# Moving the last expert's up projection ahead of the down projection before it, in a routed mixture stage on one Trainium2 core

## The reference

```
aff  = softmax(t @ w_r);  gate, idx = top_k(aff.T, cap)
xe   = t[idx]
hid  = silu(xe @ w_gate[e]) * (xe @ w_up[e])
ye   = (hid @ w_down[e]) * gate
out  = zeros.at[idx].add(ye)
```

## Time and profile before

| | |
|---|---|
| median of 3 runs | 2408.3 us (2407.99 to 2409.02) |
| profiled execution, first to last instruction | 2406.4 us |
| TensorE busy | 2205.8 us |
| VectorE busy | 1613.7 us |
| ScalarE busy | 1261.6 us |
| mean granted TensorE clock | 0.957 of full |

### The profile page before, as it was taken

One profiled execution on the slowest core, in us unless ns is written; L12 is line 12 of the kernel. 1 busy time (PEld: TensorE's weight loads), 2 busy tenths in 40 slices (PEclk: granted clock), 3 DMA queues, 4 the chain that ended last, 5 costly groups with the idle time before them and its releaser, 6 DMA issues. The chain is left out here.

```text
span 2406.4 us, 32340 instructions
## 1 busy us (share of the span) xinstructions
PE 2205.8 (92%) x11028; PEld 1677.9 (70%) x11028; DVE 1613.7 (67%) x1832; ACT 1261.6 (52%) x1486; POOL 545.4 (23%) x430
## 2 busy tenths in 40 slices
PE   8899998969999999977899999969969999999993
PEld 5677776747777777746788888757756777777772
DVE  3566664578888888855566566552258888888883
ACT  3444443157777777743443434341107777777772
POOL 1100000012234233205232222200000332344222
PEclk9999998979999999987999999989979999999997
DMA  7000004769999999934111112152169999999983
GB/s 264 1 14 8 13 14 156 280 228 378 385 385 378 396 382 383 351 95 135 36 49 49 49 48 61 56 191 88 70 245 342 382 381 389 390 380 383 393 295 126
DMA packets 169530, 520.40 MB, mean 216 GB/s; under 512 B 11808, under 2 KB 49440, under 8 KB 169184
## 3 DMA queue, kind: packets, MB, share of 16 engines
q1 hardware_dynamic: 162272, 494.05, 54.4%
q0 software_dynamic: 7168, 25.17, 4.5%
HBM read 481.43 MB, written 37.75 MB: 216 GB/s over the span
## 5 line engine op out<-in xcount | busy, mean ns | idle before, releaser
L1764 DVE TENSOR_TENSOR m_w_lo<-s_raw,m_w_hi 128x2048 fp32r<-128x2048 f32 x384 | 865.9, 2288 | 144.6 <-ACT m_w_hi L1713 143.0
L1713 ACT ACTIVATE m_w_hi<-s_raw 128x2048 fp32r<-128x2048 f32 x384 | 731.1, 1916 | 175.9 <-PE m_ps_down L1809 77.3
L1807 PE MATMUL m_ps_gate<-m_w_hi,m_xeT_hi 128*96 128x512 f32 x512 | 206.0, 402 | 3.8 <-DVE m_xeT_lo L1770 3.8
L1807 PE MATMUL m_ps_down<-m_w_hi,m_hidT_hi 128*96 128x512 f32 x512 | 203.9, 398 | 3.8 <-DVE m_hidT_lo L1770 3.8
L1809 PE MATMUL m_ps_gate<-m_w_hi,m_xeT_lo 128*96 128x512 f32 x512 | 204.3, 399 | 0.0
L1809 PE MATMUL m_ps_down<-m_w_hi,m_hidT_lo 128*96 128x512 f32 x512 | 204.1, 399 | 0.0
L1807 PE MATMUL m_ps_up<-m_w_hi,m_xeT_hi 128*96 128x512 f32 x512 | 203.9, 398 | 0.0
L1684 POOL DMA_INDIRECT acc<-m_ye,m_row_scatter x32 | 47.0, 1469 | 688.4 <-ACT m_ye L1730 688.4
L1809 PE MATMUL m_ps_up<-m_w_hi,m_xeT_lo 128*96 128x512 f32 x512 | 202.7, 396 | 0.0
L1808 PE MATMUL m_ps_gate<-m_w_lo,m_xeT_hi 128*96 128x512 f32 x512 | 202.5, 395 | 0.0
L1808 PE MATMUL m_ps_down<-m_w_lo,m_hidT_hi 128*96 128x512 f32 x512 | 202.3, 395 | 0.0
(11 more groups left out here) (228 smaller groups left out, 4200.4 us busy)
## 6 DMA issues: line engine op xcount, KB each, us to landing
s_raw<-in_w_gate SPq DMA_DIRECT2D x128, 1024.0 KB, 7.6
s_raw<-in_w_up SPq DMA_DIRECT2D x128, 1024.0 KB, 7.3
s_raw<-in_w_down SPq DMA_DIRECT2D x128, 1024.0 KB, 7.8
s_raw<-in_w_qkv_b SPq DMA_DIRECT2D x16, 512.0 KB, 5.8
s_raw<-in_w_qkv_b SPq DMA_DIRECT2D x32, 256.0 KB, 6.1
s_raw<-in_w_o_b SPq DMA_DIRECT2D x1, 8192.0 KB, 23.2
acc<-o_x SPq DMA_DIRECT2D x12, 512.0 KB, 2.6
xn<-o_xn SPq DMA_DIRECT2D x12, 512.0 KB, 3.0
```

The lines of the kernel that those rows point to most:

```text
L1713: act.activation(hi[:, split, :, :].rearrange("p k n -> p (k n)"), raw[:, slot, :], ACT.Copy).then_inc(hi_ready, 1)
L1764: dve.tensor_tensor(lo[:, split, :, :].rearrange("p k n -> p (k n)"), raw[:, slot, :], hi[:, split, :, :].rearrange("p k n -> p (k n)"), A ...
L1807: pe.matmul(out[:, cols], left_hi[:, k, :], hi[:, split, kk, cols], start=(k == 0), stop=False)
```

## The change

The order of the pieces at the end becomes: up 14, gate 15, up 15, down 14, down 15. Expert 14's list has 16 pieces now and expert 15's four. The gate is already one expert ahead, so up 15 uses the same transposed tokens as gate 15 did. `hid` of expert 15 is made on VectorE behind the split of place 13 of that list (the second piece of down 14); TensorE transposes it ahead of place 14, and ScalarE and VectorE evacuate it behind the split of place 14. The transposed `hid` of expert 14 is still in use by then, so that of expert 15 goes to the buffer of the transposed tokens of parity 0, and down 15 reads it there. `down_out(14)` keeps its place index 3 in the list of expert 15, which now is the fourth piece of down 15. The loads follow the new order: up 15 ahead of down 14, and down 15 when the pieces of down 14 have been split. Both layers have the change.

```diff
+        def before_last(e):
+            return isinstance(e, int) and e == LAST - 1
+        UP, GATE, DOWN = list(range(0, 4)), list(range(4, 8)), list(range(8, 12))
         def pieces(e):
-            slots = [0, 1, 2, 3, 8, 9, 10, 11] if is_last(e) else list(range(SLOTS))
-            return list(enumerate(slots))
+            slots = UP + GATE + (UP if before_last(e) else []) + DOWN
+            return list(enumerate(DOWN if is_last(e) else slots))
         def q_of(e, place):
-            return e * SLOTS + 4 + place
+            return e * SLOTS + 4 + place + (4 if is_last(e) else 0)
...
                 for j in range(4):
                     wait_low(sp, e - 1, j)
                     load(e, io.w_up, j, 0)
-                if not is_last(e):
+                for j in range(4):
+                    wait_low(sp, e - 1, 4 + j)
+                    load(e + 1, io.w_gate, j, 4)
+                if before_last(e):
                     for j in range(4):
-                        wait_low(sp, e - 1, 4 + j)
-                        load(e + 1, io.w_gate, j, 4)
+                        wait_low(sp, e, j)
+                        load(LAST, io.w_up, j, 0)
                 for j in range(4):
                     wait_low(sp, e - 1, 8 + j)
                     load(e, io.w_down, j, 8)
-            with sp.Fori(1, LAST) as e:
+            with sp.Fori(1, LAST - 1) as e:
                 step(e)
-            step(LAST)
+            step(LAST - 1)
+            for j in range(4):
+                wait_low(sp, LAST - 1, 12 + j)
+                load(LAST, io.w_down, j, 8)
...
@@ ScalarE
-                    ahead = 1 if 4 <= slot < 8 else 0
+                    ahead = 1 if 4 <= slot < 8 or (slot < 4 and place >= 8) else 0
                     high(q_of(e, place), (4 + place) % SPLITS, slot, (e + ahead) * 16 + base + 16)
...
-                    if place == (5 if is_last(e) else 8):
-                        turned(hidT_hi[:, :, :], e * 2 + (2 if is_last(e) else 3))
+                    if place == 8:
+                        turned(hidT_hi[:, :, :], e * 2 + 3)
                     if place == 10:
                         gate_out(e + 1, q_of(e, 8))
+                    if before_last(e) and place == 14:
+                        turned(xeT_hi[:, 0, :, :], 2 * EXPERTS)
                 if is_last(e):
-                    down_out(e, q_of(e, 8))
+                    down_out(e, q_of(e, 4))
...
@@ VectorE
-                    if place == 5:
+                    if place == 5 and not is_last(e):
                         dve.wait_ge(silu_ready, e + 1)
...
-                    if place == (5 if is_last(e) else 8):
-                        turned(hidT_lo[:, :, :], hidT_hi[:, :, :], e * 2 + (2 if is_last(e) else 3))
+                    if place == 8:
+                        turned(hidT_lo[:, :, :], hidT_hi[:, :, :], e * 2 + 3)
+                    if before_last(e) and place == 13:
+                        dve.wait_ge(silu_ready, EXPERTS)
+                        dve.wait_ge(split_used, q_of(e, 12))
+                        dve.wait_ge(T_done, 2 * LAST + 1)
+                        dve.tensor_tensor(hid[:, :], silu[:, :], up_ps[:, :], ALU.mult).then_inc(hid_ready, 1)
+                    if before_last(e) and place == 14:
+                        turned(xeT_lo[:, 0, :, :], xeT_hi[:, 0, :, :], 2 * EXPERTS)
...
@@ TensorE
+                    up_of_last = before_last(e) and slot < 4 and place >= 8
                     if slot == 0:
-                        wait(pe, hid_ready, e)
+                        wait(pe, hid_ready, e + 1 if up_of_last else e)
...
                     if slot == 8:
                         if not (isinstance(e, int) and e == 0):
                             pe.wait_ge(ye_ready, e)
-                        if is_last(e):
-                            pe.wait_ge(hid_ready, e + 1)
-                            turn(hid, e * 2 + 1)
                         pe.wait_ge(T_lo, e * 2 + (2 if is_last(e) else 3))
-                    if slot == 1 and not is_last(e):
+                    if slot == 1 and not is_last(e) and not up_of_last:
...
+                    if before_last(e) and slot == 10:
+                        pe.wait_ge(hid_ready, EXPERTS)
+                        turn(hid, 2 * LAST + 1)
                     wait_low(pe, e, place)
                     q = q_of(e, place)
-                    if slot < 4:
+                    if up_of_last:
+                        products(up_ps, xeT_hi[:, 1 - parity], xeT_lo[:, 1 - parity], slot, split, q)
+                    elif slot < 4:
                         products(up_ps, xeT_hi[:, parity], xeT_lo[:, parity], slot, split, q)
...
+                    elif is_last(e):
+                        products(down_ps, xeT_hi[:, 0], xeT_lo[:, 0], slot - 8, split, q)
```

## The result

The change makes the kernel slower: a median of 2419.95 us over four runs (2417.67 to 2421.34) against 2408.39 us over four runs of the kernel before (2407.99 to 2409.02), ratio 1.0047, 95% interval 1.0033 to 1.0062. The profiled execution has a span of 2417.4 us, 11.0 us more than the one of before.

What follows compares the result with a forecast made beforehand. TensorE was taken to bound the expert loop. Two layers at 3.84 us plus 0.7 for the clock gave 8.4 us on the 2406.4 us span, 2414.8, so a median of 2416.7 us, 0.35% slower; range 2411.9 to 2420.5.

Steps and rivals of the forecast that it cites:

- What it removes: Gap behind up 15: of 4.32 us a layer, 3.71 go, 0.61 of transposes stay; perhaps low clock, 2.46 and 1.63.
- Place 15: Last piece of down 14: hid's evacuations ahead of its split make TensorE lose 2.47 us a layer.
- The accumulator and the load: Before down 15: a late load delays ScalarE's copy of down 14, which frees the shared PSUM tile; 5.08 us lost.
- D0: First of down 15's four pieces; forecast to start at about 1059.1, 3.84 us later than before.
- P12: First of down 14's four pieces; forecast to start at 1039.82, as up 15 did before.
- The clock: Half clock behind the gap before down 15: 2.4 us a layer, bounds nothing and 3.4; net +0.7 us against before.
- What stays: Counts of products, splits, loads, scatters; down 14's loads issue some 20 us later, in by 1028, at no cost.
- D3: Last of down 15's four pieces; its load forecast to land at 1056.02, holding ScalarE idle about 1.7 us.
- The sum: Both layers' ends: 2 x 3.84 us at full clock plus 0.7 for the clock, 8.4 us slower.
- The load hidden: Before down 15: its last load lands by 1054.4; total +4.9 us, 2413.2 us; chance 0.07.
- the clock up: Behind both gaps at the layer's end the clock stays full; total +3.6 us, 2411.9 us; chance 0.05.
- The faster rival: Before down 15: copy of down 14 is covered, no gap opens; 6.6 us faster, 2401.7 us; chance 0.04.

Runs made afterwards that it cites:

- e1_evac_late: Changed kernel with the evacuations of the last transposed hid one piece later, behind the split of down 14's last piece; 2408.82 us, 0.9996 of the kernel before.
- e5_load_early: Changed kernel with down 15 loaded into the slots of gate 15, all lists in the same order; 2415.08 us, 1.0018 of the kernel before.
- e3_copy_first: Changed kernel with ScalarE's copy of down 14 ahead of the high half of down 15's last piece; 2406.0 us, 0.9982 of the kernel before.
- e7_gate_only: Changed kernel with down 15 written into the gate's PSUM tile, without the wait for the copy of down 14; 2405.22 us, 0.9978 of the kernel before.
- e6_warm: Changed kernel with 20 extra matmuls of 512 columns in the gap before down 15; 2413.63 us, 1.0016 of the kernel before.
- e8_before_warm: Kernel before the change with 14 extra matmuls of 512 columns in the gap of its last expert; 2406.75 us, 0.9986 of the kernel before.
- The second comparison: Changed kernel unaltered, run again, 7 runs against 29 of the kernel before; 2418.44 us against 2410.65, ratio 1.0032 (1.0021 to 1.0044).
- e2_evac_copy: Changed kernel with the edits of e1_evac_late and e3_copy_first together; 2402.86 us, 0.9969 of the kernel before.
- the first four experiments: First group of follow-up kernels; the kernel before, run beside them 29 times, took 2404.02 to 2413.66 us, median 2410.65.

## Why the prediction was right

The time, 2419.95 us, lies inside the stated range, 3 us above the 2416.7 forecast, and the forecast case is the one that came. Point by point:

- **What it removes.** The transposes of hid moved into down 14 and cost 0.61 us there; the gap behind up 15 is gone. Right.
- **Place 15.** Predicted 2.47 us, measured 2.41 in both layers. e1_evac_late shows the cause: with the evacuations one piece later the gap goes.
- **The accumulator and the load.** D0 was put 19.25 us after P12 (1059.07 less 1039.82) and came at 19.23. ScalarE's wait for the load was put at 1.7 us and is 1.81; the load's 4.8 us to landing came again. The bound without the load's wait (1057.35, 17.5 us) is what e5_load_early measured, and e3_copy_first and e7_gate_only show that the copy of down 14, and the single tile behind it, set D0. By the Trainium skill's fit for the GpSimd path ("DMA: Bandwidth & Descriptors", Anatomy of one DMA) the load would take an estimated 4.4 us; the trace shows 4.8 again, and the measurement decides.
- **The clock.** Taken as 2.4 us a layer, measured 2.36 and 2.33. e6_warm and e8_before_warm show that it is the idle stretch that costs this. That agrees with what the Trainium skill ("TensorE: Matmul & The Clock Gate", Part 1) says of an idle and a busy state: with the gaps filled the rows show 1.00 where they showed 0.50. That the pick between 0 and 3.4 fell so close is in part luck: behind one and the same gap of 3.2 us e5_load_early lost 1.54 us in one layer and 2.83 in the other.
- **What stays.** Down 14's loads went out some 20 us later and held nobody up: no load but D3's ended an idle stretch at the ends. In layer 0 the last of them was in at 1028.89; 1028 had been worked out. The scatter of expert 14 was hidden: its rows were free at 1066.15, 7.1 us ahead of the last copy; 5 had been expected.
- **The sum.** 8.4 us was forecast for the two ends, and 8.15 is what they give. The other 3.2 us by which the median is over the forecast are not in the sum at all. In the profile 2.5 us of them came between the two expert stages. The second comparison puts the change at 7.8 us, against a kernel before whose median is there 2.3 us higher than in the first, which speaks for scatter; that the stretch was longer in every profile with the new order speaks for a part of the change that the prediction put at nothing. The runs don't decide it. The time is 0.55 us below the top of the range, and the room up there was meant for a lower clock and a later landing, neither of which came: that the number still lies inside is luck in this part.
- **Rivals.** The load hidden, and the clock up, had the right prices for cases that did not come by themselves: e5_load_early and e6_warm made them, with ends 4.4 and 3.9 us above those of before (4.9 and 3.6 had been worked out). The faster rival, a covered copy, is e7_gate_only, which needed another accumulator for it. Its D0 is level with P15's end, as worked out, and the ends win 5.6 us (6.6 had been worked out; the last copies' waits for the scatter, 0.54 and 0.38 us, are most of the difference).

## What to carry to other kernels

When a dependent step is moved between the pieces of a pipeline, check the lead of its evacuations in the list of every engine that has them: here they stood two pieces behind the transposes everywhere but in the new place, where one piece more was enough (e1_evac_late), and that one piece held the split, the next load and, through it, a copy on which TensorE waited. Two uses of one accumulator that become neighbours need a second tile or the copy early in its engine's list; look for a tile that is already free, as the gate's was here. And a gap of some microseconds in a stream of matmuls can cost more than its length (behind those of 3.2 us and more before D0 half clock cost another 1.5 to 2.8 us, behind those of 1.9 us and less nothing), so it pays to close it fully or, failing that, to fill it.

## What the runs showed of the hardware

How long the clock stays at half of full speed around a gap was not a matter of the gap's length alone in these profiles, of which there is one for each kernel. At the gaps of 4.9 us it was low four times out of four, for 6.8 us, the first 1.8 to 2.0 of them still in the gap; at those of 3.7 us (e1_evac_late) for 3.4 us in both layers; at those of 3.2 us (e5_load_early) once for 3.4 and once for 6.8 us; at those of 1.9 us and less before D0 (e2_evac_copy, e3_copy_first) never in four. But behind 2.41 us before P15 it was low once in twelve. The kernel before, whose first four runs lay within 1.03 us, spread over 9.6 us in the 29 runs beside the first four experiments, so that 0.1% here takes many runs, while the two profiles of the changed kernel agree in the sum of both ends to 0.02 us.
